# Every second weight load of an expert issued by ScalarE, ahead of the rounding of the chunk in front

## The reference, cut to what matters

```python
top_logit, top_idx = lax.top_k(logits, TOP_K)          # 2 of 8 experts per token
for e in range(N_EXPERTS):
    out = out + gate[:, e:e + 1] * swiglu(t, w_gate[e], w_up[e], w_down[e])
# swiglu(u, g, up, d) = (silu(u @ g) * (u @ up)) @ d ; D_MODEL 1024, D_EXPERT 3584, all float32
```

## Time and profile before

| | |
|---|---|
| median of 3 runs | 1657.75 us (1656.53 to 1658.16) |
| the profiled execution | 1658.17 us, of which its span is 1656.4 us |
| PE busy | 1571.4 us, 95% of the span |
| DVE busy | 1293.3 us, 78% |
| ACT busy | 1028.5 us, 62% |
| DMA, mean over the span | 265 GB/s, 439.70 MB |

### The profile page before, as it was taken

The page is one execution under the profiler, slowest core; times in us unless marked ns, Lnnn a source line. Parts: engine busy times, 40 slices in busy tenths (PEclk is TensorE's granted clock), DMA queues, the critical chain, the costliest instruction groups (busy, mean ns, idle before and its releaser), DMA issues.

```text
span 1656.4 us, 21473 instructions
## 1 busy us (share of the span) xinstructions
PE 1571.4 (95%) x8127; PEld 1331.4 (80%) x8127; DVE 1293.3 (78%) x1102; ACT 1028.5 (62%) x865; POOL 17.9 (1%) x36
## 2 busy tenths in 40 slices
PE   5997999999799779999999999999999999999996
PEld 4986788887788668888888888888888888888885
DVE  4976744448686577888888888888888889889885
ACT  3545543346354636777677677677677677677663
POOL 4000000000000000000000000000000000000000
PEclk9998999999899879999999999999999999999998
DMA  7431365555344038999999999999999999999970
GB/s 232 152 128 51 110 207 200 178 178 179 126 128 140 7 115 304 376 339 358 375 339 358 375 340 358 374 341 356 375 343 356 374 342 357 374 341 358 371 277 25
DMA packets 203182, 439.70 MB, mean 265 GB/s; under 512 B 12088, under 2 KB 31104, under 8 KB 203136
## 3 DMA queue, kind: packets, MB, share of 16 engines
q1 hardware_dynamic: 200080, 437.38, 74.6%
q10 hardware_dynamic: 3056, 1.68, 0.4%
HBM read 437.98 MB, written 1.05 MB: 265 GB/s over the span
## 4 chain that ended last, share of the span: by engine, by line
PE 85%; DVE 8%; ACT 3%; SPq 2%; issue 1%; DMA 0%; DVEq 0%; ACTq 0%
PE bank L1335 26%; PE bank L1337 25%; PE bank L1336 25%; DVE wlo L803 2%; PE bank L1670 2%; PE bank L1708 1%; PE bank L1412 1%; SPq L396 1%; PE bank L1330 1%; PE bank L1486 1%; PE bank L1687 0%; ACT work L577 0%; PE bank L1688 0%; PE bank L1475 0%; ACT whi L520 0%
## 5 line engine op out<-in xcount | busy, mean ns | idle before, releaser
L803 DVE TENSOR_TENSOR wlo<-raw,whi 128x2048 fp32r<-128x2048 f32 x415 | 935.8, 2287 | 150.4 <-ACT whi L708 93.3
L708 ACT ACTIVATE whi<-raw 128x2048 fp32r<-128x2048 f32 x341 | 633.0, 1910 | 13.4 <-DMA raw<-in_w_exp_down_dram 10.0
L1335 PE MATMUL bank<-whi,uTh 128*128 128x512 f32 (+1 forms) x1312 | 517.2, 394 | 5.7 <-DVE uTl L865 4.7
L1337 PE MATMUL bank<-whi,uTl 128*128 128x512 f32 (+1 forms) x1312 | 510.1, 389 | 0.0
L1336 PE MATMUL bank<-wlo,uTh 128*128 128x512 f32 (+1 forms) x1312 | 509.4, 388 | 0.0
L1335 PEld LDWEIGHTS bank<-whi,uTh 128*128 128x128 f32 x1312 | 247.8, 189 | 55.7 <-issue 5.0
L1337 PEld LDWEIGHTS bank<-whi,uTl 128*128 128x128 f32 x1312 | 247.5, 189 | 51.6
L1336 PEld LDWEIGHTS bank<-wlo,uTh 128*128 128x128 f32 x1312 | 248.0, 189 | 48.5
L1335 PE MATMUL bank<-whi,hTr 128*128 128x512 f32 x528 | 206.1, 390 | 0.0
L1336 PE MATMUL bank<-wlo,hTr 128*128 128x512 f32 x528 | 205.5, 389 | 0.0
L1337 PE MATMUL bank<-whi,hTr 128*128 128x512 f32 x528 | 205.5, 389 | 0.0
(11 more groups left out here) (247 smaller groups left out, 1161.5 us busy)
## 6 DMA issues: line engine op xcount, KB each, us to landing
raw<-in_w_exp_gate_dram SPq DMA_DIRECT2D x112, 1024.0 KB, 5.2
raw<-in_w_exp_up_dram SPq DMA_DIRECT2D x112, 1024.0 KB, 5.2
raw<-in_w_exp_down_dram SPq DMA_DIRECT2D x112, 1024.0 KB, 4.9
raw<-in_w_in_dram SPq DMA_DIRECT2D x28, 1024.0 KB, 5.4
raw<-in_w_ffn_gate_dram SPq DMA_DIRECT2D x11, 1024.0 KB, 5.1
raw<-in_w_ffn_up_dram SPq DMA_DIRECT2D x11, 1024.0 KB, 5.2
raw<-in_w_ffn_down_dram SPq DMA_DIRECT2D x11, 1024.0 KB, 5.0
raw<-in_w_out_dram SPq DMA_DIRECT2D x8, 1024.0 KB, 5.0
```

The lines of the kernel that those rows point to most:

```text
L708: nc.scalar.activation(whi[:, s % SPLIT, :], raw[:, s % RAW, :], ACT.Copy).then_inc(hi_a, 1)
L803: return V.tensor_tensor(wlo[:, n % RAW, :], raw[:, n % RAW, :], whi[:, n % SPLIT, :].bitcast(F32), ALU.subtract).then_inc(lo_ready, 1)
L1335: T.matmul(o, sth, mvh, start=start, stop=False)
L1337: return T.matmul(o, stl, mvh, start=False, stop=stop)
```

## The change

An item's loads 5, 7, 9, ..., 41 (19 of 42) are taken out of SP's list. ACT issues them from its own queue: in step n, for even n from 0 to 36, it waits for chunk n - 2 to be consumed and issues the load of chunk n + 5, ahead of the rounding of chunk n + 4 and behind the other things of the step. ACT reads the expert's number from the table at the head of each item. Slots, semaphores and the sizes of the transfers are as before.

```diff
+BY_ACT = range(LEAD + 1, EXP_LOADS, 2)
...
+        def expert_chunk(n, e):
+
+            kind, r, hf = EXP_ORDER[n]
+            if kind == "d":
+                r0 = r * NC + hf * 2 * P
+                src = w_exp_down[0, bass.ds(e, 1), r0:r0 + 2 * P, :]
+            else:
+                w = w_exp_gate if kind == "g" else w_exp_up
+                src = w[0, bass.ds(e, 1), hf * HALF * P:(hf + 1) * HALF * P, r * NC:(r + 1) * NC]
+            return as_k(raw[:, (NSTATIC + n) % RAW, :], 2 if kind == "d" else HALF), src.rearrange("a (k p) n -> p (a k) n", p=P)
...
-                for n, (kind, r, hf) in enumerate(EXP_ORDER):
+                for n in range(EXP_LOADS):
+                    if n in BY_ACT:
+                        continue
                     sp.wait_ge(consumed, i * EXP_LOADS + (NSTATIC + n - RAW + 1))
...
+                    to, src = expert_chunk(n, e)
+                    sp.dma_start(to, src).then_inc(filled[(NSTATIC + n) % RAW], 16)
...
+            def load_next(n, i, e):
+
+                act.wait_ge(consumed, i * EXP_LOADS + (NSTATIC + n - RAW + 1))
+                to, src = expert_chunk(n, e)
+                act.dma_start(to, src).then_inc(filled[(NSTATIC + n) % RAW], 16)
+
             with act.Fori(0, n_items) as i:
+                e = act.value_load(item_expert[0:1, bass.ds(i, 1)], min_val=0, max_val=NE - 1)
                 for n, (kind, r, hf) in enumerate(EXP_ORDER):
...
+                    if n + LEAD + 1 in BY_ACT:
+                        load_next(n + LEAD + 1, i, e)
                     hi(n + LEAD, i)
```

## The result

The changed kernel takes 1818.32 us (median of 4 runs, 1814.49 to 1827.33), the kernel before 1657.14 us in the same comparison. The ratio is 1.0985, 95% interval 1.0941 to 1.1029: 161 us slower. The forecast of slower held; the predicted 1722 us and the range up to 1800 did not. The profiled execution has a span of 1812.4 us against 1656.4.

A forecast was written before the change was run, and what follows sets the result against it. PE was taken to bound the expert loop, with DMA right behind. Eight items, each losing 5.0 us in rounds and 3.0 at its end, gave 64 us on 1658.17: predicted 1722 us, range 1680 to 1800.

The forecast's parts named there:

- the last interval: Item's end, turn at chunk 34 to 39: 15.8 us before, chain 2.0 us too long plus 1.0 for sharing, 3.0 per item.
- a round: Expert loop, turn to turn: 17.8 us against PE's 16.8, so PE waits 1.0 us for `exh`.
- the item's start: Loads 5 and 7 after the item before: covered by other ACT work, 0; 1.4 us per item without that slack.
- what binds: Expert loop: PE sets the pace, busy 940 of 940 us, with DMA right behind at a share of 0.99.
- the sign: Whole kernel: slower 0.89, same 0.08, faster 0.03.
- Rival C: ACT's queue: loads not held back by unmet waits, so time stays 1658 us within 2; chance 0.09.
- load 41 sharing: Item's end: load 41 goes out with SP's 43 while 42 is under way, losing 0 to 2.8 us; 1.0 taken.
- The chain of 17.8: Turn to turn: two ACT loads in a row, two roundings, a subtraction, `exh`, the turn; 2L + 7.6, L being issue to landing.
- the sum of the rounds: Five intervals between an item's six turns, chunks 4 to 34: 1.0 us each, 5.0 per item, over 8 items.
- A, worse sharing: SP's and ACT's loads lock together in flight and land later: L = 6.5, 198 us, 1856 in all; chance 0.2.
- B, the clock: PE idling at item ends lowers its granted clock: 28 us in all, 1750; chance 0.13.
- The rule on issuing engines: Skill page: DMAs of different issuing engines interleave on the same 16 engines; gain only 0.37 us issue time per load.

The follow-up runs named there:

- b3: Changed kernel, but ACT issues loads 7, 9, ..., 41 one step sooner, at the moment SP had issued them: 1657.5 us, ratio 0.9999.
- b1: Changed kernel with SP's even-chunk expert loads cut to a quarter of the bytes: 1803.7 us, ratio 1.0883.
- a1: Changed kernel, but ACT issues its load at the head of the step, ahead of the turn and the silu's wait: 1814.45 us, ratio 1.0972.
- a3: Changed kernel, but ACT issues only loads 11, 17, 23, 29, 35 and 41 of each item, SP the rest: 1855.35 us, ratio 1.1199.
- c3: Changed kernel with ten more products on PE ahead of its wait for the item's last turn: 1809.52 us, ratio 1.0904.
- b4: Kernel a3 with SP's even-chunk loads cut to a quarter of the bytes: 1670.81 us, ratio 1.0083.

## Why the prediction was wrong, step by step

The forecast was 64 us, and the turns account for 157: the five intervals inside an item 100 for 40, the boundary 35 for 0, the last interval 22 for 24. So two terms of the sum failed: a round was priced at 1.0 us and lost 2.5 on average, and the item's start was priced at nothing.

**Right: what binds, and the sign.** PE had no idle time to give back, the odd loads went out behind unmet waits and not before, and 18 of the issues cost nothing on ACT (b3). Rival C, that ACT's loads aren't held back, fell: in the rows above each went out 0.14 to 0.22 us after the start of the ACTIVATE in front of it, and none of the 152 ahead of it.

**Right in number, in part by luck: the last interval.** 3.0 us forecast, 2.7 measured, 22 us in all against 24. But 1.0 of the forecast was for load 41 sharing, and it landed after 5.3 us (median of 8), 0.2 over the 5.1 reckoned; the chain came out longer instead.

**Mis-sized: the round.** The chain of 17.8 is 18.6 in the round shown. From its rows, each load up to the start of its rounding, forecast in brackets: turn to issue 0.14 (0.2), load 5.14 (5.1), to the next issue 0.22 (0.1), load 5.29 (5.1), from there to `exh` 6.36 (5.99: 3.74 + 2.33 less the overlap of 0.08), `exh` 0.68 (0.68), to ACT's start on the next turn 0.75 (0.65). Half of the miss is one link that I read wrongly: I let the subtraction of 18 start at the end of its rounding, but DVE is still at that of 17, and two subtractions (4.49 us) outlast a rounding and one subtraction. So an undisturbed round loses 1.8, not 1.0.

**Mis-sized by far: the sum of the rounds.** Forecast 8 x 5.0 = 40 us, measured 100. An undisturbed 1.8 would make 72. The other 28 are in round 1, which lost 2.6 and not 1.8, and in rounds with longer landings (up to 8.2 us) or a lowered clock; how they divide was not tested. The forecast took one clean round for all.

**Wrong: the item's start costs nothing.** The prediction had load 5 land 5.1 us after its issue, just in time for its rounding, and priced the start at 0; measured are 5.1 us for each boundary. The boundary after:

```profile
1194.73 1.09 ACT L726 ACTIVATE uTh<-bank 128x512 fp32r<-128x512 f32 x2 [4.50 <-PE bank L1353]
1195.88 0.39 ACTq L754 DMA_DIRECT2D raw<-in_w_exp_gate_dram  x1
...
1203.21 1.92 ACT L715 ACTIVATE whi<-raw 128x2048 fp32r<-128x2048 f32 x1 [1.66 <-DMA raw<-in_w_exp_gate_dram]
1203.43 0.38 ACTq L754 DMA_DIRECT2D raw<-in_w_exp_down_dram  x1
...
1213.72 0.60 ACT L624 ACTIVATE hTr<-bank 128x512 fp32r<-128x512 f32 x1 [2.32 <-PE bank L1724]
```

```profile
1194.73 0.37 SPq L418 DMA_DIRECT2D raw<-in_w_exp_down_dram  x1
```

SP sends load 6 when the last chunk is consumed, ACT sends load 5 after the same wait, 1.15 us later. SP's lands after 4.9 us, its load 8 goes out at 1200.17, and ACT's lands after 7.2 us, two later than forecast; at the seven boundaries load 5 takes 6.9 to 7.2 us. I weighed such a meeting for load 41 and not for load 5, though both engines' waits for the same event stood in the code. Behind it the rounding of 7 starts at 1209.50, and DVE's additions to h (L1282), in order behind subtractions, hold PE's next products into the bank that they read (25.2 us in 16 waits, L1703). Giving loads 5 and 7 back to SP (a2) returned 22 of the boundaries' 35 us, so these two loads are most of it; the other 13 were not taken apart.

**The rivals.** A, worse sharing, was priced at L = 6.5 for all loads and 1856 us; the median of ACT's loads is 5.2 (4.9 to 8.2), and b1's rounds stay at 18.6 with hardly anything to share, so it is not what makes the rounds of the changed kernel slow. But it is real: it made a1 as slow as the change, and a3 slower. B, the clock, was priced at 28 us. Here is one case of it, after the wait for the last turn that ended at 1183.5:

```profile
1177.00:1184.00 7.00, 4.89 (x33) 4.28 (x32) 5.57 (x4) 4.37 (x4) 0.00 (x0) 1.00 1.05 387
1184.60:1191.40 6.80, 6.80 (x24) 5.74 (x23) 5.85 (x5) 5.64 (x4) 0.00 (x0) 0.52 0.27 100
```

Intervals with such a stretch are longer by 2.0 us in the rounds (7 of them) and 3.9 at the boundary (5 of 7), together some 34 us. That is a difference between intervals, not an experiment: a longer wait may cause both, and c3 didn't part them. An estimate from the stretch of the loop says about as much: a mean of 0.97 over 1090 us is 33 us of PE's work at the upper level, 20% of the loss, and more than that the lowered clock did not cost PE directly. How much of it was on the path stays open.

**The rule on issuing engines.** The Trainium skill ("DMA: Bandwidth & Descriptors", section "Issuing engines are not separate DMA queues") has DMAs of all issuing engines interleave on the same 16 engines, saving only issue time. b3 agrees on the gain: 0.9999 with 18 of 42 loads moved. a3 and b4 show what it means for one load of ACT's that goes out with one of SP's: it lands after 8.8 us (median) where SP's is whole and after 5.5 where it is a quarter.

## What to carry to other kernels

A DMA put on a compute engine's queue takes over every unmet wait that stands before it on that engine: ask which event releases it, not how long the issue takes, and follow that event until the chain meets itself. Where two engines issue and wait for the same count of a semaphore, the transfers start together and one or both land late (5.9 and 9.3 us in a3, 7.8 and 7.2 in a1), and where the stream is as dense as here the loads behind them do too. And a forecast from the clean round alone came out too low here: boundaries, where every engine waits for the same last chunk, need their own sum.

## What the runs showed of the hardware that was not expected

ACT's sequencer issued a DMA 0.14 to 0.22 us after the start of the ACTIVATE in front in the rounds shown, on a busy engine too (1006.75 during L624), and b3 shows that such issues cost nothing. Two loads of 1 MiB that go out together on different queues were not delayed alike: in a3 SP's, issued at 1018.13, took 5.9 us and ACT's, issued 0.14 us later, 9.3; in a1 SP's, issued at 1015.34, took 7.8 and ACT's, issued 0.12 us later, 7.2, so that it landed first. One such meeting in a3 was followed by four loads of one queue, 2.5 to 2.9 us apart, that took 7.5 to 7.8 us each. And late loads cost without any meeting: c2, with every load due two chunks later and landing in about 5 us, lost 222 us. Its rounds 2 to 5 grew by 3.1 us on average (20.0 against 16.9), its boundary by 7.6, and PE's granted clock has a mean of 0.94 in the loop.
